# An expert stage's gate and up products in blocks of 512 columns, its 1 MB weight chunks loaded as one transfer of 2 KB rows, and a job's begin in another order

## What is computed

```python
def swiglu(h, w1, w3, w2):
    return (jax.nn.silu(h @ w1) * (h @ w3)) @ w2

def moe_swiglu(h, w_router, w1, w3, w2):
    logits = jnp.einsum('bsd,de->bse', h.astype(jnp.float32), w_router.astype(jnp.float32))
    top_v, top_i = lax.top_k(logits, TOP_K_EXPERTS)
    top_w = jax.nn.softmax(top_v, axis=-1)
    gate = jnp.sum(jax.nn.one_hot(top_i, N_EXPERTS, dtype=jnp.float32) * top_w[..., None], axis=-2)
    ...
    for e in range(N_EXPERTS):
        y = y + gate[..., e:e + 1] * swiglu(h, w1[e], w3[e], w2[e])
```

## Time and profile before

| | us |
|---|---|
| median of 3 runs | 1559.25 (1557.99 to 1559.93) |
| profiled execution, whole | 1560.89 |
| its span, first to last instruction | 1558.9 |
| TensorE busy | 1501.7 (96%) |
| VectorE busy | 1241.6 (80%) |
| ScalarE busy | 1051.4 (67%) |
| loads on SP's queue, share of 16 engines | 83.5% |
| bytes moved, mean rate | 466.29 MB, 299 GB/s |
| DMA packets, under 2 KB | 334875, 269800 |

### The profile page before, as it was taken

The page is one execution under the profiler, slowest core; times in us unless marked ns, Lnnn a source line. Parts: engine busy times, 40 slices in busy tenths (PEclk is TensorE's granted clock), DMA queues, the critical chain, the costliest instruction groups (busy, mean ns, idle before and its releaser), DMA issues.

```text
span 1558.9 us, 21888 instructions
## 1 busy us (share of the span) xinstructions
PE 1501.7 (96%) x6973; PEld 1230.8 (79%) x6973; DVE 1241.6 (80%) x1264; ACT 1051.4 (67%) x1153; POOL 16.1 (1%) x17
## 2 busy tenths in 40 slices
PE   7999999999999999999999999999999999999994
PEld 6888888788888778878878878877887887887883
DVE  5885655446885779889889888898889988988987
ACT  5555544336556567777787787687688778778774
POOL 0000000000000010000000000000000000000001
PEclk9999999999999989999999999999999999999997
DMA  9953665257553599899899999999999999989985
GB/s 372 329 177 110 196 193 189 94 187 257 201 170 109 175 345 339 267 388 385 314 391 385 338 380 385 339 357 386 384 329 386 394 322 386 389 321 387 385 321 203
DMA packets 334875, 466.29 MB, mean 299 GB/s; under 512 B 14784, under 2 KB 269800, under 8 KB 334840
## 3 DMA queue, kind: packets, MB, share of 16 engines
q1 hardware_dynamic: 333120, 459.49, 83.5%
q0 software_dynamic: 1632, 6.33, 1.1%
q10 hardware_dynamic: 88, 0.02, 0.0%
HBM read 450.05 MB, written 15.73 MB: 299 GB/s over the span
## 4 chain that ended last, share of the span: by engine, by line
issue 63%; PE 33%; DVE 1%; DMA 1%; POOL 1%; ACT 0%; POOLq 0%; SPq 0%; ACTq 0%; DVEq 0%
PE bank L793 10%; PE bank L795 10%; PE bank L794 10%; PE bank L875 1%; DMA w_raw<-in_w_in 1%; PE bank L819 1%; POOL x_by_slot L460 0%; PE bank L1094 0%; PE bank L859 0%; DMA y_first_choice<-y_by_slot,row_of_choice 0%; PE bank L930 0%; PE bank L1007 0%; PE bank L910 0%; PE bank L847 0%; PE bank L938 0%
## 5 line engine op out<-in xcount | busy, mean ns | idle before, releaser
L1173 DVE TENSOR_TENSOR w_lo<-w_raw,w_hi 128x1024 fp32r<-128x1024 f32 (+1 forms) x448 | 780.8, 1757 | 107.0 <-ACT w_hi L491 89.4
L491 ACT ACTIVATE w_hi<-w_raw 128x1024 fp32r<-128x1024 f32 (+1 forms) x448 | 663.6, 1492 | 130.2 <-PE bank L795 108.9
L793 PE MATMUL bank<-w_hi,hT_hi 128*128 128x512 f32 (+1 forms) x1424 | 569.1, 400 | 4.6 <-DVE w_lo L1168 2.2
L795 PE MATMUL bank<-w_hi,hT_lo 128*128 128x512 f32 (+1 forms) x1424 | 555.6, 390 | 0.0
L794 PE MATMUL bank<-w_lo,hT_hi 128*128 128x512 f32 (+1 forms) x1424 | 554.4, 389 | 0.0
L793 PEld LDWEIGHTS bank<-w_hi,hT_hi 128*128 128x128 f32 x1424 | 269.3, 189 | 61.1 <-issue 4.8
L795 PEld LDWEIGHTS bank<-w_hi,hT_lo 128*128 128x128 f32 x1424 | 269.1, 189 | 57.4
L794 PEld LDWEIGHTS bank<-w_lo,hT_hi 128*128 128x128 f32 x1424 | 269.8, 189 | 50.7
L485 ACT ACTIVATE w_hi<-w_raw 128x2048 fp32r<-128x2048 f32 (+2 forms) x100 | 169.7, 1699 | 159.5 <-PE bank L795 152.8
L1168 DVE TENSOR_TENSOR w_lo<-w_raw,w_hi 128x2048 fp32r<-128x2048 f32 (+2 forms) x100 | 201.5, 2019 | 95.1 <-ACT w_hi L485 94.3
L793 PE MATMUL bank<-w_hi,hiddenM_hi 128*128 128x512 f32 x448 | 176.8, 395 | 2.1 <-DVE w_lo L1173 2.1
(11 more groups left out here) (232 smaller groups left out, 843.9 us busy)
## 6 DMA issues: line engine op xcount, KB each, us to landing
w_raw<-in_moe_w SPq DMA_DIRECT2D x672, 512.0 KB
w_raw<-in_w_in SPq DMA_DIRECT2D x64, 512.0 KB
w_raw<-in_dense_w SPq DMA_DIRECT2D x44, 512.0 KB
w_raw<-in_dense_w SPq DMA_DIRECT2D x44, 256.0 KB
w_raw<-in_w_out SPq DMA_DIRECT2D x16, 512.0 KB
x_by_slot<-x_residual SPq DMA_DIRECT2D x12, 512.0 KB, 10.9
w_raw<-in_w_pool_proj SPq DMA_DIRECT2D x8, 512.0 KB
w_raw<-in_w_attn_proj SPq DMA_DIRECT2D x8, 512.0 KB
```

Source lines behind the costliest of these rows:

```text
L491: act.activation(whi[:, m % SLOTS, 0:n], raw8[m % 8][:, 0:n], ACT.Copy).then_inc(s_hi, 1)
L793: pe.matmul(dst, ahi, bhi, start=start, stop=False)
L795: return pe.matmul(dst, alo, bhi, start=False, stop=stop)
L1173: dve.tensor_tensor(wlo[:, m % SLOTS, 0:n], raw8[m % 8][:, 0:n], whi[:, m % SLOTS, 0:n], ALU.subtract).then_inc(s_lo, 1)
```

## The change

An up block has 512 columns of the hidden row instead of 256, so there are seven, each of four chunks: two of `w1` (512 of its 1024 rows each), then two of `w3`. A chunk is one transfer with 2 KB rows. The gate product goes to bank 4 and the up product to bank 5, each as two chunks. SiLU, product, `hiddenM_hi` and `hiddenM_lo` work on 512 columns; the transposes of a block are four and stand behind the first two chunks of the next block. `hiddenM` has one buffer, so SiLU waits for the transposes of the block before. ScalarE and VectorE run two splits of a block, then SiLU (ScalarE) or the low part of the last block (VectorE), and so on as the diff has it; its parts are, in order, SP's, ScalarE's, TensorE's and VectorE's. The dummy SiLU moves ahead of the loop over jobs, the wait for the scatter to the SiLU of block 0, and the copies of the result behind the split of chunk 3.

```diff
-NB_E = FFE // 256
+NB_E = FFE // 512
-JOB_CHUNKS = 2 * NB_E + KC_E
+JOB_CHUNKS = 4 * NB_E + KC_E
...
             def up_chunk(m, e, g):
                 t = raw8[m % 8].rearrange("p (k n) -> p k n", n=512)
-                for j, w in enumerate((w1, w3)):
-                    src = w[bass.ds(e * D + (m % 2) * 512, 512), bass.ds(g * 512 + (m % 4 // 2) * 256, 256)]
-                    sp.dma_start(t[:, :, 256 * j:256 * j + 256],
-                                 src.rearrange("(k p) n -> p k n", p=P)).then_inc(s_ld[m % 8], 16)
+                v = (w1, w3)[m % 4 // 2][bass.ds(e * D + (m % 2) * 512, 512), bass.ds(g * 512, 512)
+                                         ].rearrange("(k p) n -> p k n", p=P)
+                sp.dma_start(t, v).then_inc(s_ld[m % 8], 32)
...
+            act.activation(silu0[:], cst[:, C_ONE:C_ONE + 1], ACT.Silu)
             with act.Fori(0, njobs) as i:
                 j8 = i * (JOB_CHUNKS // 8)
-                act.activation(silu0[:], cst[:, C_ONE:C_ONE + 1], ACT.Silu)
...
+                def silu_m(b, first):
+                    act.wait_ge(s_use, i * JOB_CHUNKS + b * 4 + (MOE0 + 2))
+                    if not first:
+                        act.wait_ge(m_ft, i * NB_E + b)
+                    act.activation(hsM[:], bank[4][:], ACT.Silu).then_inc(m_si, 1)
...
+                def up_block(p, n, more=0, dyn=0, first=False):
+                    m = 4 * p + LOOK
+                    b = more + p
+                    split_m(m, n, j8 + dyn)
+                    split_m(m + 1, n, j8 + dyn)
+                    if first:
+                        act.wait_ge(s_xsc, 2 * TT * 16)
+                    silu_m(b, first)
+                    if not first:
+                        hid_hi_m(b - 1, (p - 1) % 2)
+                    split_m(m + 2, n, j8 + dyn)
+                    split_m(m + 3, n, j8 + dyn)
...
                 for k in range(24, 27):
                     split_m(d0 + k, FULL, j8)
+                split_m(d0 + 27, FULL, j8)
                 act.wait_ge(s_use, i * JOB_CHUNKS + (MOE0 + JOB_CHUNKS))
                 act.wait_ge(s_ys, i * 16 + 16)
                 for j in range(2):
                     act.activation(ysb[:, 512 * j:512 * j + 512], bank[6 + j][:], ACT.Copy).then_inc(m_y, 1)
-                split_m(d0 + 27, FULL, j8)
...
+                def up_block(b, dyn, q, first=False):
+                    for j in range(2):
+                        if not first:
+                            pe.wait_ge((m_si, m_hm)[j], i * NB_E + b)
+                        for h in range(2):
+                            chunk(MOE0 + 2 * j + h, [bank[4 + j][:]], hehi, helo, 4 * h, 512, h == 0, h == 1, dyn, tiles=1)
+                        if j == 0 and not first:
+                            pe.wait_ge(m_flo, i * NB_E + b - 2 + LEAD)
+                            hiddenT_m(b - 1, 1 - q)
...
+                def mul_m(b):
+                    dve.wait_ge(m_si, i * NB_E + b + 1)
+                    dve.wait_ge(s_use, i * JOB_CHUNKS + b * 4 + (MOE0 + 4))
+                    dve.tensor_tensor(hsM[:], hsM[:], bank[5][:], ALU.mult).then_inc(m_hm, 1)
...
+                def up_block(b, n):
+                    m = 4 * b + LOOK
+                    split_m(m, n, j8)
+                    split_m(m + 1, n, j8)
+                    if b:
+                        hid_lo_m(b - 1, (b - 1) % 2)
+                    split_m(m + 2, n, j8)
+                    mul_m(b)
+                    split_m(m + 3, n, j8)
```

More of the change, by code:

```diff
@@ L167, in build @@
         hidMlo = sb("hiddenM_lo", [P, KC_E, P], FR, moe)
-        hsM = sb("hiddenM", [P, 2, 256], F32, moe)
-        lgT = hsM[0:E, 0, :]
+        hsM = sb("hiddenM", [P, 512], F32, moe)
+        lgT = hsM[0:E, 0:S]
         selR = sb("select", [P, TT, P], FR, moe)
@@ L745, in hid_hi_m @@
                 def hid_hi_m(b, q):
                     act.wait_ge(m_ft, i * NB_E + b + 1)
-                    dst = hidMhi[:, 2 * b:2 * b + 2, :] if isinstance(b, int) else hidMhi[:, bass.ds(b * 2, 2), :]
-                    act.activation(dst, bank[q][:, 0:256].rearrange("p (k t) -> p k t", t=P),
-                                   ACT.Copy).then_inc(m_fhi, 1)
-                def pair(p, n, more=0, dyn=0, first=False):
-                    for u in range(2):
-                        m = 4 * p + 2 * u + LOOK
-                        b = more * 2 + (2 * p + u)
-                        split_m(m, n, j8 + dyn)
-                        if not (first and u == 0):
-                            hid_hi_m(b - 1, 1 - u)
-                        if first and u == 1:
-                            act.wait_ge(s_xsc, 2 * TT * 16)
-                        silu_m(b, u)
-                        split_m(m + 1, n, j8 + dyn)
@@ L771, in _ @@
+                up_block(0, FULL, first=True)
+                with act.Fori(0, 2) as it:
+                    up_block(1, FULL, it * 2, it)
+                    up_block(2, FULL, it * 2, it)
+                up_block(5, FULL)
+                up_block(6, HALF)
+                d0 = 4 * NB_E + LOOK
                 for k in range(4):
@@ L1115, in hiddenT_m @@
                     pe.wait_ge(m_hm, i * NB_E + b + 1)
-                    for f in range(2):
-                        ins = pe.transpose(bank[q][:, f * P:f * P + P], hsM[:, q, f * P:f * P + P], ident)
+                    for f in range(4):
+                        ins = pe.transpose(bank[q][:, f * P:f * P + P], hsM[:, f * P:f * P + P], ident)
                     ins.then_inc(m_ft, 1)
-                def pair(it, first=False):
-                    for u in range(2):
-                        c = MOE0 + 2 * u
-                        b = it * 2 + u
-                        if not first:
-                            pe.wait_ge(m_hm, i * NB_E + b - 1)
-                        chunk(c, [bank[4 + u][:]], hehi, helo, 0, 512, True, False, i * jd + it, tiles=1)
-                        if not (first and u == 0):
-                            if not first:
-                                pe.wait_ge(m_flo, i * NB_E + b - 2 + LEAD)
-                            hiddenT_m(b - 1, 1 - u)
-                        chunk(c + 1, [bank[4 + u][:]], hehi, helo, 4, 512, False, True, i * jd + it, tiles=1)
-                pe.wait_ge(s_glo, i * 2 + 2)
-                pair(0, first=True)
-                with pe.Fori(1, NB_E // 2) as it:
-                    pair(it)
+                def up_block(b, dyn, q, first=False):
[7 more added lines that the diff above has]
+                            hiddenT_m(b - 1, 1 - q)
+                pe.wait_ge(s_glo, i * 2 + 2)
+                up_block(0, i * jd, 0, first=True)
+                up_block(1, i * jd + 1, 1)
+                with pe.Fori(1, 3) as it:
+                    for u in range(2):
+                        up_block(it * 2 + u, i * jd + (it * 2 + u), u)
+                up_block(NB_E - 1, i * jd + (NB_E - 1), 0)
                 gather(i + 1)
                 for k in range(KC_E):
-                    c = MOE0 + 2 * NB_E + k
+                    c = MOE0 + 4 * NB_E + k
                     if k == 4:
```

38 lines of the change are left out of this document (9 added, 29 removed).

## The result

The changed kernel takes 1540.69 us (median of 4 runs, 1540.63 to 1542.82), the kernel before 1559.59 us beside it (4 runs, 1557.99 to 1561.21). The ratio is 0.9878, with a 95% interval of 0.9866 to 0.989: 18.9 us, 1.2%, faster. The profiled execution took 1542.82 us, of which the span is 1541.0; that of before 1560.89 and 1558.9. Two terms of the sum had the wrong size, the gain in the jobs (step 3) and the cost at the end (step 7).

What follows compares the result with a forecast made beforehand. TensorE was taken to set the pace, DMA close behind. Terms -21.3 (jobs), +0.4 (inside jobs), +1.9 and +1.5 (first job), +1.8 (end) sum to -15.7: from 1560.89 to 1545.2, forecast 1545 us, range 1541 to 1551.

Steps and rivals of the forecast that it cites:

- step 3: Seven later expert jobs: without stalls each takes 120.1 us, so 21.3 us of stalls, low clock and unevenness are gained.
- step 7: Kernel's end: result copies wait behind a dummy split of chunk 3, so store, gathers and output come 1.8 us later.
- Step 1: Up-block weight loads: 2 KB rows bring 1 MB in 2.6 us instead of 2.72, bounds 2.5 to 3.07.
- slower loads: Rival, chance 0.06: up loads of the new shape run at 341 GB/s, a job takes 123.6 us, total some 1567.
- Step 2: Job's begin: both stalls go; SiLU of block 0 has 0.6 us in hand, the product 1 us.
- the stall moves: Rival, chance 0.15: TensorE waits for SiLU of block 0 at a job's begin; 5 to 8 us lost, 1550 to 1553.
- step 4: Inside a job: SiLU and product stay off the path; the wait behind the gathered rows grows 0.05 a job, +0.4 total.
- Step 5: First job: the moved scatter guard makes a 3.5 us stall before chunk 4, +1.9, plus 1.5 for low clock.
- Step 6: SiLU's table load, ahead of the loop over jobs: loads go from eight to one.
- The rival: Chance 0.05: a table load stays in each job ahead of SiLU of block 0, a 0.7 us stall in seven jobs, 1550.

## Where the prediction was right, and which of its terms failed

**The bound and the main term.** That TensorE sets the pace and that the stall at the job's begin is the place was right, and both rivals for its cause fell. The condition under which the gain is kept, loads that follow, held: the DMA share in the jobs is 0.99.

**Step 1, the loads.** 2.6 us per MB were taken, 2.57 measured; the upper bound of 3.07 and with it the rival "slower loads" fell. The mixed stretch of rows ahead of the stage, worked out for its 2 KB part, was the right neighbour. The Trainium skill ("DMA: Bandwidth & Descriptors", Specifications) would have had no gain from rows above 512 B; 385 became 409 GB/s, so the measurement stands against it. But the gain in the rate was worth little by itself (2.7 us with the new blocks).

**Step 2, the new begin.** Right in kind, timid in size: SiLU at T + 9.2, not 10.3; the product at T + 14.2, not 15.4. The whole chain of loads stands about 1 us earlier against T than was worked out from the old job (hi of chunk 5 starts at T + 6.8, not 7.8); the cause is open. So the margin ahead of the rival "the stall moves" was 1.7 us and not 0.6. With 1 KB rows this rival's stall did show, at 1.2 us in total.

**Step 3, what it is worth, was the first term that was mis-sized.** It took 120.1 us for a job without stalls, and no lower end for that. A job takes 119.73, with step 4's 0.05 in it: 0.4 less, 2.9 us over seven jobs. The 120.1 was the fifth job's length less the stalls I had found. One part of the difference is seen: a pair of old blocks took 11.41 us, from the transposes of one block to those of the next but one, on TensorE's timeline of before,

```profile
1203.67 0.38 PE L1117 MATMUL bank<-shape_constants,hiddenM 128*128 128x128 f32 x2
...
1215.08 0.38 PE L1117 MATMUL bank<-shape_constants,hiddenM 128*128 128x128 f32 x2
```

and one new block 11.39 us, on that of after:

```profile
1177.63 0.60 PE L1118 MATMUL bank<-shape_constants,hiddenM 128*128 128x128 f32 x4
1189.02 0.60 PE L1118 MATMUL bank<-shape_constants,hiddenM 128*128 128x128 f32 x4
```

Four transposes in one group cost some 0.03 us less than two groups of two (the mean of these distances over the jobs), 0.2 us over seven blocks. Another 0.1 lies right behind the two stalls of the old job: there a pair of transposes took 0.44 us and not the 0.38 shown here. The rest, about 0.1 us, I have not found.

**Step 4, inside a job.** Right: no wait for SiLU or product. The waits at the ninth down chunk, seven of the 14, stayed at 0.3 us.

**Step 5, the first job,** was the right place with the wrong size: +3.4 forecast, +5.2 measured. Against T the stall's parts are: last matmul of chunk 3 as forecast; the guard opens 0.53 us later than before (T + 15.09 against 14.56), and 0.16 us pass from the forecast end of SiLU to the matmul; the low clock lasts 6.8 us and costs 2.9, where 3.4 us and 1.5 were taken. That makes +5.5, less the 0.4 by which this job, too, is shorter. The step left out that the length of the low stretch is not a constant, and that the landing of a scatter varies.

**Step 6, the table load.** Right: one load for 56 SiLU in a loop of eight passes. The Trainium skill ("ScalarE activation tables: per-element evaluation and per-set limits", Table sets in the compiler and the runtime) has loads placed per block of code; this trace shows none in the loop's body. The rival would have cost nothing either: with the load in every job the jobs took 119.73 us.

**Step 7, the end, was the second term that was mis-sized,** and the one that failed in kind: +1.8 forecast, +0.1 measured. "Nothing covers it" was the wrong sentence. The copies did move by 1.8 us against the last matmul (1523.30 - 1519.73 = 3.57, before 1539.52 - 1537.75 = 1.77) and the gather's begin with them. But the first gather got back 1.1 us by no longer standing beside a split. The remaining 0.6 us came back behind the gathers' instructions: before, the third gather began at 1547.36 and the addition that reads it started at 1553.26; after, 1530.01 and at most 1535.18. The other traces show the same. In five kernels with the copies early the last gather instruction ends 11.8 us behind the last matmul, in the five with the copies late 12.5 to 12.6. From the last matmul to the end are 20.8 to 21.7 us (mean 21.3) in the first five and 21.3 to 21.7 (mean 21.5) in the others. The lowest and the highest are of two kernels with the same order here, so this stretch varies by 0.9 us by itself; what brings the last 0.5 us back was not tested. The cue stood in the trace of before: GpSimd's gathers of the same size took 2.09, 0.96 and 0.94 us there, and I did not ask why the first was long.

**The sum.** -2.9 (jobs), -1.7 (end), +1.8 (first job), +0.5 (the stage begins later; over the eleven kernels it begins at 553.7 to 554.7) are -2.3: 1545.2 - 2.3 = 1542.9, and the profiled execution took 1542.82. The median lies another 2.1 us below it, where I had let it be equal: the other three executions took 1540.63 to 1540.74, and their spans, 1538.8 to 1538.9, show that this one execution was the long one; why is open. The time fell out of the range by these 2.1 us together with steps 3 and 7. The range's low end, 1541, took the gain in the jobs as bounded by the stalls found. Its working, 1559.25 - 21.3 + 3.7, also left out the 0.4 of step 4; with it the end would have been 1542, and the miss larger. An allowance of half a microsecond per job, for what the inventory of waits did not hold, would have covered the result.

## What to carry to other kernels

When a consumer is late because an in-order engine does one long piece of work ahead of it, a larger block that moves the moment at which it is wanted can be worth more than faster loads or a shorter queue: here it brought nearly all of the 19 us with either of these beside it, and each of these without it 2 or 3. When a wait that happens once moves to an earlier place in the work, work out the stall there with the low clock behind it; here moving it behind SiLU of block 0 was worth 7 us in the traces and 5 in the medians. Account for a loop's steady length in full before using it as a base, and put what is left over into the range.

## What the runs showed of the hardware

**An indirect transfer on GpSimd waits for VectorE's split.** The split has two inputs in SBUF. An indirect transfer that started 0.06 to 1.05 us into one ended 0.82 to 0.91 us behind the split's end, and the others took 0.93 to 1.00 us. The Trainium skill ("SBUF — State Buffer", SBUF: two separate sides) says that VectorE instructions with two SBUF inputs contend with GpSimd instructions that read SBUF, and that whichever starts first holds the port while the other fully blocks. The traces agree where VectorE was first. Where GpSimd was first, by 0.07 us or by 0.33 us, both took their usual time (0.95 and 2.29 us), so no blocking of VectorE is seen. The traces show the timing alone; that a port is the reason is the page's account, and no run here tested it.

**The low clock behind a stall has different lengths.** In the kernel before, and in the one with wide rows and the old blocks, four stalls of 2.61 to 3.04 us from start to start were followed by 3.4 us at 0.50, and three of 2.66 to 2.76 by none; behind those of 4.42 us (the changed kernel) and 4.78 us (the old begin with the new blocks) the clock was at 0.50 for 6.8 us; behind 2.17 us it stayed at 1.00. Which it is can't be told from the length alone.
